# Moving the operands of the large products to start at 128 modulo 256 bytes, in a mixer and feed-forward kernel

## The chip, the cores and the metric

One core of one Trainium2 chip runs the kernel. The metric is the device time of one execution in microseconds (us); lower is better.

## What is computed

The reference is two blocks in a row on 512 tokens of width 1024, in float32. The first block normalises x (with 16 meta tokens in front), projects it, mixes it by a pooling mixer and by gated linear attention, and adds a mixture of 16 experts. The second block has two layers, each a gated feed-forward product, a hybrid attention mixer and a second feed-forward product:

```python
def swiglu(x, w_gate, w_up, w_down):
    return (jax.nn.silu(x @ w_gate) * (x @ w_up)) @ w_down
for l in range(DEPTH_2):
    x = x + 0.5 * swiglu(rms_norm(x, norm_ffn1[l]), ffn1_w_gate[l], ffn1_w_up[l], ffn1_w_down[l])
    x = x + hybrid_mixer(rms_norm(x, norm_mix[l]), w_in[l], w_proj_dil[l], w_proj_sb[l],
                         w_out[l], cos, sin)
    x = x + 0.5 * swiglu(rms_norm(x, norm_ffn2[l]), ffn2_w_gate[l], ffn2_w_up[l], ffn2_w_down[l])
return rms_norm(x, norm_final)
```

The feed-forward width is 2816, the input projection of each mixer is 1024 x 5120.

## The kernel before

The activations lie feature-major: a tile has 128 features on the partitions, 8 chunks c of them, and 512 tokens along the free dimension. Every large product is made from split operands: a float32 value is stored as a rounded part (`_hi`) and the rest (`_lo`), and the product is three matmuls, hi by hi, lo by hi and hi by lo, added in one PSUM bank. ScalarE makes the rounded part, VectorE the rest, for weights (`w_hi`, `w_lo`, a ring of three panels; lines 509 and 514) and for activations alike.

`product` (lines 547 to 560) is a panel of 128 output features: for each of 8 chunks c three matmuls, with a 128x128 piece of the weights stationary and a row of 512 tokens moving, 24 matmuls in all, called **wide** here. Its moving operands are `xg_hi`/`xg_lo` (the scaled x), `hid_hi_ff`/`hid_lo_ff` (the hidden layer), `y_hi`/`y_lo` (the gated sum in the second mixer), `heads_hi`/`heads_lo` (its attention outputs), and in the first mixer `y1_hi`/`y1_lo`, which the profile prints as `y_hi` and `y_lo` too. TensorE runs the panels in the fixed order of `weight_order`; each waits on a semaphore for its `w_lo`.

In the feed-forward stages 71 pairs of gate and up panels are made with seven half-size products instead of eight (`seven_pe` and `piece`, line 1866). Each of the seven is 4 chunks by three matmuls, with 256 tokens moving, called **narrow** here: 84 narrow matmuls per pair. Four of the seven take sums of quarters of x (`xs_hi`, `xs_lo`) as moving operand, three take quarters of `xg_hi`, `xg_lo` (`x_quarter`); three of the four and one of the three have sums of weights (`ws_hi`, `ws_lo`) stationary, the rest plain weights from the ring.

In the first block, the mixture of experts (`panel_products`, matmul at line 1347) has the roles swapped: weights from `w_hi`, `w_lo` move, 512 wide, and token tiles are stationary.

`sb(...)` allocates SBUF in the order in which the buffers are written down, each right behind the last, rounded up to 32 bytes; a buffer in an `ExitStack` that has been closed gives its place to what follows. So the start of each operand in a partition's memory is fixed by the sizes of all that stands before it. `xg_hi` and `xg_lo` have rows of L = 528 numbers (16 meta tokens and 512 tokens, 2112 bytes), of which all stages behind the first mixer read from column META = 16 on.

Start of the operands, in bytes modulo 256, worked out from the allocation:

| operand | before | after the change |
|---|---|---|
| `w_hi`, `w_lo`, stationary (pieces 512 bytes apart) | 128 | 128 |
| `xg_hi`, `xg_lo` from the token columns, chunk c (rows of 2112 bytes) | 192, 0, 64, 128, and again | 128 for every c (rows of 2048) |
| `hid_*_ff`, `xs_*`, `ws_*`, second mixer's `y_*` and `heads_*` | 224 | 128 |
| first mixer's `y1_*`; token tiles of the experts | 128 | 128 |

Of the kernel before, what the change touches and what calls it, by code (L numbers as in the profile page):

```python
# [159 lines left out]
def build(nc, dram, out, counts, final):  # L160
# [4 lines left out]
    with stack:  # L165
# [28 lines left out]
        x = sb(stack, "x", [P, DC, T])  # L194
        xg_hi = sb(stack, "xg_hi", [P, DC, L], F32R)
        xg_lo = sb(stack, "xg_lo", [P, DC, L], F32R)
        rstd = sb(stack, "rstd", [P, T])
# [58 lines left out]


        with ExitStack() as phase:

            weight_diag = sb(phase, "weight_diag", [P, TB, TOP_K, P])  # L260
# [3 lines left out]
        first_rstd = sb(stack, "first_rstd", [P, T])  # L264
        gain_pair = sb(stack, "gain_pair", [P, 2 * DC])


        with ExitStack() as phase:
            slot_of = sb(phase, "slot_of", [P, TB, TOP_K], U32)
            token_of = sb(phase, "token_of", [P, TILES], U32)  # L270
            weight = sb(phase, "weight", [P, TOP_K, TB, 1])
            with ExitStack() as ring:
                expert_raw = sb(ring, "expert_raw", [P, EXPERT_OWN, PANEL])
# [288 lines left out]
        def x_product(pe, key, emptied_by, emptied_key, ready=None, banks=l_banks):  # L562
            bank = claim(pe, banks, key, emptied_by, emptied_key)
            cols = panel_shape(panel_of[key])[1]
            product(pe, key, [bank[0:cols, :]], lambda c: [xg_hi[:, c, META:]], lambda c: [xg_lo[:, c, META:]], ready)

# [47 lines left out]
        def round_x(act, stage, c, factor):  # L614
            act.activation(xg_hi[:, c, META:], x[:, c, :], ACT.Copy, scale=factor).then_inc(*x_hi.done((stage, c)))

        def rest_of_x(dve, stage, c, factor):
            dve.wait_ge(*x_hi.upto((stage, c)))
            dve.scalar_tensor_tensor(xg_lo[:, c, META:], x[:, c, :], factor, xg_hi[:, c, META:].bitcast(F32),
                                     ALU.mult, ALU.subtract).then_inc(*x_lo.done((stage, c)))  # L620
# [25 lines left out]

        half = L // 2

        def mixer_1_pe(pe):
            def both(key, ready=None):  # L650

                l = claim(pe, l_banks, key, taken, (key, "l"))
                t = claim(pe, t_banks, key, taken, (key, "t"))
                product(pe, key, [l[:, 0:half], t[:, 0:half]],
                        lambda c: [xg_hi[:, c, 0:half], xg_hi[:, c, half:]],
                        lambda c: [xg_lo[:, c, 0:half], xg_lo[:, c, half:]], ready)

# [108 lines left out]
        def route_chunk(pe, c):  # L766

            w_high, w_low = split_memory(panel_of["route", 0])
            if c == 0:
                pe.wait_ge(*panel_lo.upto(panel_of["route", 0]))  # L770
                pe.wait_ge(*shaped.upto(("carry", N_CHUNK - 2, 1)))
            pe.wait_ge(*x_lo.upto(("m1", c)))
            for n, (w, part) in enumerate(((w_high, xg_hi), (w_high, xg_lo), (w_low, xg_hi))):
                m = pe.matmul(bank_s[:, 0, :], w[:, c * P:(c + 1) * P], part[:, c, META:],
                              start=c == 0 and n == 0, stop=c == DC - 1 and n == 2)
            if c == DC - 1:
                m.then_inc(*used.done(panel_of["route", 0]))

        def mixer_1_act(act):
            load_log_and_exp(act)  # L780
            act.wait_ge(*shaped.upto("meta_g"))
            round_value(act, "meta", xg_hi[:, :, 0:META], meta_g[:, :, :])
            act.wait_ge(loaded["gains"], 16)
# [103 lines left out]
        def mixer_1_dve(dve):  # L887
# [5 lines left out]
                "p (c o) -> p c o", o=1).to_broadcast([P, DC, META]), ALU.mult).then_inc(*shaped.done("meta_g"))  # L893
            rest_of_value(dve, "meta", xg_lo[:, :, 0:META], xg_hi[:, :, 0:META], meta_g[:, :, :])
            for c in range(DC):
# [10 lines left out]
            def take_both(key, dst, n=P):  # L906
                dve.wait_ge(*used.upto(panel_of[key]))
                dve.tensor_tensor(dst[0:n, 0:half], l_banks.of(key)[0:n, 0:half], all_rstd[0:n, 0:half],
                                  ALU.mult).then_inc(*taken.done((key, "l")))
                dve.tensor_tensor(dst[0:n, half:], t_banks.of(key)[0:n, 0:half], all_rstd[0:n, half:],  # L910
                                  ALU.mult).then_inc(*taken.done((key, "t")))
# [806 lines left out]
        def normalise_between_act(act):  # L1718
            load_log_and_exp(act)
            act.wait_ge(*shaped.upto("gain_pair"))  # L1720
            for half in range(2):
                ts = half_columns(half)
                for c in range(DC):
                    if c % 4 == 0:
                        act.wait_ge(*x_new.upto(("moe", 2 * half + 1, c // 4)))
                    act.activation(xg_hi[:, c, META:][:, ts], x[:, c, ts], ACT.Copy,
                                   scale=gain_pair[:, DC + c:DC + c + 1]).then_inc(
                        *x_hi.done(("n", c) if half else ("n_first_half", c)))
# [28 lines left out]
        def normalise_half_dve(dve, half, chunks):  # L1757
            ts = half_columns(half)
            for c in chunks:
                key = ("n", c) if half else ("n_first_half", c)  # L1760
                dve.wait_ge(*x_hi.upto(key))
                dve.scalar_tensor_tensor(xg_lo[:, c, META:][:, ts], x[:, c, ts], gain_pair[:, DC + c:DC + c + 1],
                                         xg_hi[:, c, META:][:, ts].bitcast(F32), ALU.mult, ALU.subtract).then_inc(
                    *x_lo.done(key))
# [74 lines left out]
        def x_quarter(part, k, t):  # L1839
            return part[:, 4 * k:4 * k + 4, META + half_t * t:META + half_t * t + half_t]  # L1840

# [1213 lines left out]
```

## Time and profile before

| | |
|---|---|
| median of three timed runs | 2575.88 us (2571.2 to 2576.82) |
| profiled execution: span from first to last instruction | 2569.2 us |
| profiled execution's own time | not recorded apart from the span; the median stands 6.7 us above the span |
| TensorE busy | 2477.2 us (96%) |
| VectorE, ScalarE, GpSimd busy | 1706.7, 1129.6, 422.1 us |
| mean granted TensorE clock | 0.989 of 2.4 GHz |

Matmuls are pipelined, so the mean duration of one is longer than the time from its start to the next one's start; that distance, called the **step** here, is what a matmul costs in a row of matmuls. It is read from start times. A busy TensorE is not a TensorE at its peak.

### The profile page before, as it was taken

Reading aid. Unit: us, or ns where it says so; the run is one execution under the profiler, and the core shown is the slowest. Engines: PE = TensorE matmul, PEld = TensorE weight load, DVE = VectorE, ACT = ScalarE, POOL = GpSimd, SP = SyncE. Lnnn points to the kernel's source line nnn. Section 1 sums busy time; section 2 is a strip of 40 time slices with the busy share of each in tenths; the row PEclk is TensorE's granted clock in tenths of the full one; section 3 lists DMA queues with packets and bytes.
Section 4 is the critical chain, followed back from the end, with each engine's and each line's share of the span. In section 5 each row is a group of like instructions: output and inputs, shape, how many; then the busy total and the mean of one; then the engine's idle time right before and its main releaser. Section 6 shows DMA issues by size and latency. Waiting matters only on the chain. (4 is left out here: it accounts for less than half of the span.)

```text
span 2569.2 us, 38480 instructions
## 1 busy us (share of the span) xinstructions
PE 2477.2 (96%) x15217; PEld 2130.2 (83%) x15217; DVE 1706.7 (66%) x2316; ACT 1129.6 (44%) x1586; POOL 422.1 (16%) x450
## 2 busy tenths in 40 slices
PE   7997996999999999999999999999999999999998
PEld 6876775889897878778898989999887777899996
DVE  5455996658686434467696878777743436687776
ACT  4344884335343233545353454444412255544443
POOL 0002111702012400012020102111050001111110
PEclk9998998999999999999999999999999999999999
DMA  4215995246454321125564546555332212465652
GB/s 144 66 58 198 385 413 203 83 143 162 139 127 133 98 80 55 64 91 156 144 172 129 124 134 166 145 158 140 119 110 84 67 42 90 131 157 150 159 142 72
DMA packets 120713, 348.69 MB, mean 136 GB/s; under 512 B 16066, under 2 KB 21074, under 8 KB 120274
## 3 DMA queue, kind: packets, MB, share of 16 engines
q1 hardware_dynamic: 81634, 245.48, 28.5%
q0 software_dynamic: 38032, 98.06, 16.4%
q8 instruction: 125, 2.05, 0.3%
q10 hardware_dynamic: 864, 2.62, 0.3%
q14 instruction: 58, 0.48, 0.1%
HBM read 331.95 MB, written 12.58 MB: 134 GB/s over the span
## 5 line engine op out<-in xcount | busy, mean ns | idle before, releaser
L514 DVE TENSOR_TENSOR w_lo<-w_raw,w_hi 128x1024 fp32r<-128x1024 f32 (+2 forms) x353 | 422.7, 1198 | 141.2 <-ACT w_hi L509 139.5
L509 ACT ACTIVATE w_hi<-w_raw 128x1024 fp32r<-128x1024 f32 (+2 forms) x353 | 352.4, 1003 | 364.4 <-PE bank_l L558 342.4
L558 PE MATMUL bank_l<-xg_hi,w_hi 128*128 128x512 f32 (+1 forms) x1008 | 395.8, 393 | 17.5 <-DVE w_lo L514 15.5
L558 PE MATMUL bank_l<-xg_lo,w_hi 128*128 128x512 f32 (+1 forms) x1008 | 389.8, 387 | 0.0
L558 PE MATMUL bank_l<-xg_hi,w_lo 128*128 128x512 f32 (+1 forms) x1008 | 387.5, 384 | 0.0
L558 PE MATMUL bank_l<-hid_hi_ff,w_hi 128*128 128x512 f32 x704 | 279.8, 397 | 4.2 <-DVE hid_lo_ff L644 4.2
L558 PE MATMUL bank_l<-hid_hi_ff,w_lo 128*128 128x512 f32 x704 | 278.7, 396 | 0.0
L558 PE MATMUL bank_l<-hid_lo_ff,w_hi 128*128 128x512 f32 x704 | 276.6, 393 | 0.0
L2009 ACT ACTIVATE ws_hi<-ws_raw 128x1024 fp32r<-128x1024 f32 x142 | 150.6, 1061 | 276.2 <-DVE ws_raw L2131 148.7
L558 PEld LDWEIGHTS bank_l<-xg_hi,w_hi 128*128 128x128 f32 x1008 | 190.0, 189 | 64.8 <-DVE w_lo L514 15.5
L1869 PE MATMUL bank_s<-xs_hi,ws_hi 128*128 128x256 f32 x852 | 241.4, 283 | 1.0 <-DVE ws_lo L2098 1.0
L1869 PE MATMUL bank_s<-xs_lo,ws_hi 128*128 128x256 f32 x852 | 240.7, 283 | 0.0
L1869 PE MATMUL bank_s<-xs_hi,ws_lo 128*128 128x256 f32 x852 | 240.3, 282 | 0.0
L558 PEld LDWEIGHTS bank_l<-xg_lo,w_hi 128*128 128x128 f32 x1008 | 190.0, 188 | 40.4 <-issue 2.2
L558 PEld LDWEIGHTS bank_l<-xg_hi,w_lo 128*128 128x128 f32 x1008 | 190.4, 189 | 39.3
L2098 DVE TENSOR_TENSOR ws_lo<-ws_raw,ws_hi 128x1024 fp32r<-128x1024 f32 x142 | 173.9, 1225 | 46.1 <-ACT ws_hi L2009 39.1
L2258 DVE TENSOR_TENSOR val_ff<-bank_l,rstd 128x512 f32<-128x512 f32 x96 | 66.3, 691 | 152.1 <-PE bank_l L558 127.3
L1869 PEld LDWEIGHTS bank_s<-xs_hi,ws_hi 128*128 128x128 f32 x852 | 162.3, 191 | 2.2 <-DVE ws_lo L2098 1.6
L1869 PEld LDWEIGHTS bank_s<-xs_hi,ws_lo 128*128 128x128 f32 x852 | 162.8, 191 | 0.0
L1869 PEld LDWEIGHTS bank_s<-xs_lo,ws_hi 128*128 128x128 f32 x852 | 162.6, 191 | 0.0
L558 PEld LDWEIGHTS bank_l<-hid_hi_ff,w_hi 128*128 128x128 f32 x704 | 132.2, 188 | 36.2 <-DVE hid_lo_ff L644 6.3
L558 PEld LDWEIGHTS bank_l<-hid_hi_ff,w_lo 128*128 128x128 f32 x704 | 132.2, 188 | 33.1
(440 smaller groups left out, 5467.4 us busy)
## 6 DMA issues: line engine op xcount, KB each, us to landing
ws_raw<-in_ff_up POOLq DMA_DIRECT2D x213, 256.0 KB, 4.1
w_raw<-in_ff_gate SPq DMA_DIRECT2D x88, 512.0 KB
expert_raw<-in_experts SPq DMA_DIRECT2D x81, 512.0 KB, 18.7
w_raw<-in_in SPq DMA_DIRECT2D x80, 512.0 KB
w_raw<-in_ff_down SPq DMA_DIRECT2D x64, 512.0 KB
ws_raw<-in_ff_gate POOLq DMA_DIRECT2D x71, 256.0 KB, 5.5
up_raw<-in_ff_up SPq DMA_DIRECT2D x71, 256.0 KB, 2.9
w_raw<-in_out SPq DMA_DIRECT2D x24, 512.0 KB
```

What stands on the lines that cost most here:

```text
L509: act.activation(split_memory(i)[0], split_part(i), ACT.Copy).then_inc(*panel_hi.done(i))
L514: dve.tensor_tensor(lo, split_part(i), hi.bitcast(F32), ALU.subtract).then_inc(*panel_lo.done(i))
L558: done = pe.matmul(dst, w[:, c * cols:(c + 1) * cols], moving, start=c == 0 and n == 0, stop=c == kc - 1 and n == 2)
L1869: done = pe.matmul(product_at[name], w[:, c * P:(c + 1) * P], m[:, c, :], start=c == 0 and n == 0, stop=c == DC // 2 - 1 and n == 2)
L2009: act.activation(ws_hi[:, 2 * pair:2 * pair + 2, :], raw_of_two(stage, j, pair), ACT.Copy).then_inc(*ws_high.done((stage, j, pair)))
L2098: dve.tensor_tensor(ws_lo[:, both, :], raw_of_two(stage, j, pair), ws_hi[:, both, :].bitcast(F32), ALU.subtract).then_inc(*ws_low.done((st ...
L2258: dve.tensor_tensor(val[:, :], l_banks.of(key)[:, :], rstd[:, :], ALU.mult).then_inc(*shaped.done((stage, g, m)))
```

## The change

No instruction is added, removed or moved on any engine, and no wait or semaphore differs. The two products that the first mixer makes of 528 tokens are cut as 256 and 272 columns instead of 264 and 264. All else is where operands lie. The scaled x of the first mixer gets its own names `in_hi` and `in_lo` with the old rows of 2112 bytes, in a scope that is closed at once; `xg_hi` and `xg_lo` take the same place with rows of 2048 bytes, and an unused buffer `behind_xg` fills what that frees, so that what follows keeps its place. Further unused buffers (`before_spent` of 160 bytes, `behind_weight` of 96 bytes) and `gain_pair`, now ahead, push the buffers of the later stages to the offsets of the table above.

```diff
         x = sb(stack, "x", [P, DC, T])
-        xg_hi = sb(stack, "xg_hi", [P, DC, L], F32R)
-        xg_lo = sb(stack, "xg_lo", [P, DC, L], F32R)
+        with ExitStack() as opening:
+            in_hi = sb(opening, "in_hi", [P, DC, L], F32R)
+            in_lo = sb(opening, "in_lo", [P, DC, L], F32R)
+        xg_hi = sb(stack, "xg_hi", [P, DC, T], F32R)
+        xg_lo = sb(stack, "xg_lo", [P, DC, T], F32R)
+        sb(stack, "behind_xg", [P, 2 * DC * META])
...
+        gain_pair = sb(stack, "gain_pair", [P, 2 * DC])
+        sb(stack, "before_spent", [P, 40])
         with ExitStack() as phase:
...
         first_rstd = sb(stack, "first_rstd", [P, T])
-        gain_pair = sb(stack, "gain_pair", [P, 2 * DC])
...
             weight = sb(phase, "weight", [P, TOP_K, TB, 1])
+            sb(phase, "behind_weight", [P, 24])
...
         def x_product(pe, key, emptied_by, emptied_key, ready=None, banks=l_banks):
             bank = claim(pe, banks, key, emptied_by, emptied_key)
+            of_hi, of_lo = (in_hi, in_lo) if key[0] in ("q", "r") else (xg_hi, xg_lo)
             cols = panel_shape(panel_of[key])[1]
-            product(pe, key, [bank[0:cols, :]], lambda c: [xg_hi[:, c, META:]], lambda c: [xg_lo[:, c, META:]], ready)
+            product(pe, key, [bank[0:cols, :]], lambda c: [of_hi[:, c, -T:]], lambda c: [of_lo[:, c, -T:]], ready)
...
-        half = L // 2
+        half = T // 2
...
-                product(pe, key, [l[:, 0:half], t[:, 0:half]],
-                        lambda c: [xg_hi[:, c, 0:half], xg_hi[:, c, half:]],
-                        lambda c: [xg_lo[:, c, 0:half], xg_lo[:, c, half:]], ready)
+                product(pe, key, [l[:, 0:half], t[:, 0:L - half]],
+                        lambda c: [in_hi[:, c, 0:half], in_hi[:, c, half:]],
+                        lambda c: [in_lo[:, c, 0:half], in_lo[:, c, half:]], ready)
...
         def x_quarter(part, k, t):
-            return part[:, 4 * k:4 * k + 4, META + half_t * t:META + half_t * t + half_t]
+            return part[:, 4 * k:4 * k + 4, half_t * t:half_t * t + half_t]
```

The other edits put `in_hi`/`in_lo` or `xg_hi`/`xg_lo` without META where the old names with META stood.

## Rows read from the trace of the kernel before

**Rows 1.** The page: busy time and share of the engines, and the granted clock in 40 slices.
```profile
PE 2477.2 (96%) x15217; PEld 2130.2 (83%) x15217; DVE 1706.7 (66%) x2316; ACT 1129.6 (44%) x1586; POOL 422.1 (16%) x450
...
PEclk9998998999999999999999999999999999999999
```
**Rows 2.** Busy time by engine in three stretches of the second block (start:end, length, busy).
```profile
439.00:800.00 361.00, 357.88 (x2119) 314.99 (x2118) 269.59 (x337) 150.94 (x207) 93.85 (x87) 1.00 0.45 125
800.00:1150.00 350.00, 345.20 (x2089) 273.37 (x2088) 167.89 (x243) 131.70 (x196) 54.19 (x33) 1.00 0.27 85
1150.00:1510.00 360.00, 357.91 (x2314) 323.78 (x2313) 277.18 (x363) 165.47 (x229) 56.32 (x78) 1.00 0.53 140
```
**Rows 3.** TensorE's groups by line and form: busy us, mean ns, idle before.
```profile
L558 PE MATMUL bank_l<-xg_hi,w_hi 128*128 128x512 f32 x920 | 368.8, 401 | 2.0 <-DVE xg_lo L619 2.0
...
L558 PE MATMUL bank_l<-hid_hi_ff,w_hi 128*128 128x512 f32 x704 | 279.8, 397 | 4.2 <-DVE hid_lo_ff L644 4.2
...
L1869 PE MATMUL bank_s<-xs_hi,ws_hi 128*128 128x256 f32 x852 | 241.4, 283 | 1.0 <-DVE ws_lo L2098 1.0
...
L1869 PE MATMUL bank_s<-xs_hi,w_hi 128*128 128x256 f32 x284 | 80.2, 282 | 0.0
...
L558 PE MATMUL bank_l<-y_hi,w_hi 128*128 128x512 f32 x192 | 77.7, 405 | 0.4 <-DVE y_lo L644 0.4
...
L558 PE MATMUL bank_l<-heads_hi,xg_hi 128*128 128x512 f32 x32 | 13.5, 422 | 3.5 <-DVE gates L2760 2.3 <-DVE part L2796 1.1
...
L558 PE MATMUL bank_s<-xg_hi,w_hi 128*128 128x512 f32 x24 | 9.5, 396 | 2.1 <-DVE xg_lo L1762 2.1
...
L558 PE MATMUL bank_t<-xg_hi,w_hi 128*128 128x512 f32 x16 | 6.3, 392 | 0.0
```
**Rows 4.** TensorE's timeline (start us, duration us): panels of `xg`, then of `hid`.
```profile
467.08 0.40 PE L558 MATMUL bank_l<-xg_lo,w_hi 128*128 128x512 f32 x1
...
533.36 0.39 PE L558 MATMUL bank_l<-xg_hi,w_lo 128*128 128x512 f32 x1
533.59 0.40 PE L558 MATMUL bank_l<-hid_hi_ff,w_hi 128*128 128x512 f32 x1
...
578.16 0.40 PE L558 MATMUL bank_l<-hid_hi_ff,w_lo 128*128 128x512 f32 x1
```
**Rows 5.** TensorE's timeline: three output panels of the first mixer (operands `y1_*`), and what follows each.
```profile
175.11 0.40 PE L558 MATMUL bank_l<-y_hi,w_hi 128*128 128x512 f32 x1
...
180.60 0.40 PE L774 MATMUL bank_s<-xg_hi,route_parts 128*128 128x512 f32 x1
...
193.60 0.39 PE L558 MATMUL bank_l<-y_hi,w_hi 128*128 128x512 f32 x1
...
199.04 0.40 PE L774 MATMUL bank_s<-xg_hi,route_parts 128*128 128x512 f32 x1
...
205.93 0.39 PE L558 MATMUL bank_l<-y_hi,w_hi 128*128 128x512 f32 x1
...
211.39 0.39 PE L774 MATMUL bank_s<-xg_hi,route_parts 128*128 128x512 f32 x1
```
**Rows 6.** Two of these stretches: length, TensorE busy, clock, DMA share, GB/s.
```profile
175.00:181.00 6.00, 6.00 (x28) 1.00 0.38 130
...
205.00:211.00 6.00, 6.00 (x28) 1.00 0.00 0
```
**Rows 7.** TensorE's timeline: expert down products, both operands at 128.
```profile
311.35 0.39 PE L1347 MATMUL bank_s<-w_lo,ht_hi_tile 128*128 128x512 f32 x1
...
313.65 0.39 PE L1347 MATMUL bank_s<-w_hi,ht_lo_tile 128*128 128x512 f32 x1
```
**Rows 8.** TensorE's timeline: one round of 84 narrow matmuls, 48 from `xs`, then 36 from `xg`.
```profile
1685.00 0.28 PE L1869 MATMUL bank_s<-xs_hi,ws_hi 128*128 128x256 f32 x1
...
1690.73 0.28 PE L1869 MATMUL bank_t<-xg_hi,ws_hi 128*128 128x256 f32 x1
...
1694.96 0.28 PE L1869 MATMUL bank_s<-xs_hi,ws_hi 128*128 128x256 f32 x1
```

More of the change, by code:

```diff
@@ L614, in round_x @@
         def round_x(act, stage, c, factor):
-            act.activation(xg_hi[:, c, META:], x[:, c, :], ACT.Copy, scale=factor).then_inc(*x_hi.done((stage, c)))
+            act.activation((in_hi if stage == "in" else xg_hi)[:, c, -T:], x[:, c, :], ACT.Copy, scale=factor).then_inc(*x_hi.done((stage, c)))
         def rest_of_x(dve, stage, c, factor):
             dve.wait_ge(*x_hi.upto((stage, c)))
-            dve.scalar_tensor_tensor(xg_lo[:, c, META:], x[:, c, :], factor, xg_hi[:, c, META:].bitcast(F32),
+            hi, lo = (in_hi, in_lo) if stage == "in" else (xg_hi, xg_lo)
+            dve.scalar_tensor_tensor(lo[:, c, -T:], x[:, c, :], factor, hi[:, c, -T:].bitcast(F32),
                                      ALU.mult, ALU.subtract).then_inc(*x_lo.done((stage, c)))
@@ L773, in route_chunk @@
             for n, (w, part) in enumerate(((w_high, xg_hi), (w_high, xg_lo), (w_low, xg_hi))):
-                m = pe.matmul(bank_s[:, 0, :], w[:, c * P:(c + 1) * P], part[:, c, META:],
+                m = pe.matmul(bank_s[:, 0, :], w[:, c * P:(c + 1) * P], part[:, c, :],
                               start=c == 0 and n == 0, stop=c == DC - 1 and n == 2)
@@ L781, in mixer_1_act @@
             act.wait_ge(*shaped.upto("meta_g"))
-            round_value(act, "meta", xg_hi[:, :, 0:META], meta_g[:, :, :])
+            round_value(act, "meta", in_hi[:, :, 0:META], meta_g[:, :, :])
             act.wait_ge(loaded["gains"], 16)
@@ L893, in mixer_1_dve @@
                 "p (c o) -> p c o", o=1).to_broadcast([P, DC, META]), ALU.mult).then_inc(*shaped.done("meta_g"))
-            rest_of_value(dve, "meta", xg_lo[:, :, 0:META], xg_hi[:, :, 0:META], meta_g[:, :, :])
+            rest_of_value(dve, "meta", in_lo[:, :, 0:META], in_hi[:, :, 0:META], meta_g[:, :, :])
             for c in range(DC):
@@ L909, in take_both @@
                                   ALU.mult).then_inc(*taken.done((key, "l")))
-                dve.tensor_tensor(dst[0:n, half:], t_banks.of(key)[0:n, 0:half], all_rstd[0:n, half:],
+                dve.tensor_tensor(dst[0:n, half:], t_banks.of(key)[0:n, 0:L - half], all_rstd[0:n, half:],
                                   ALU.mult).then_inc(*taken.done((key, "t")))
@@ L1725, in normalise_between_act @@
                         act.wait_ge(*x_new.upto(("moe", 2 * half + 1, c // 4)))
-                    act.activation(xg_hi[:, c, META:][:, ts], x[:, c, ts], ACT.Copy,
+                    act.activation(xg_hi[:, c, ts], x[:, c, ts], ACT.Copy,
                                    scale=gain_pair[:, DC + c:DC + c + 1]).then_inc(
@@ L1761, in normalise_half_dve @@
                 dve.wait_ge(*x_hi.upto(key))
-                dve.scalar_tensor_tensor(xg_lo[:, c, META:][:, ts], x[:, c, ts], gain_pair[:, DC + c:DC + c + 1],
-                                         xg_hi[:, c, META:][:, ts].bitcast(F32), ALU.mult, ALU.subtract).then_inc(
+                dve.scalar_tensor_tensor(xg_lo[:, c, ts], x[:, c, ts], gain_pair[:, DC + c:DC + c + 1],
+                                         xg_hi[:, c, ts].bitcast(F32), ALU.mult, ALU.subtract).then_inc(
                     *x_lo.done(key))
```

## The prediction

> **What bounds the kernel now.** I read the page first, then busy time by stretches, then start times. TensorE is busy 2477.2 of 2569.2 us, and the granted clock is at its upper level, 2.4 GHz, in nearly every slice [rows 1]. In the second block, from 439 us to the end, the reader is to see how little room there is beside it: 357.88 busy of 361.00 us, 345.20 of 350.00 and 357.91 of 360.00, at a clock of 1.00, while VectorE, the next engine, has 277.18 of 360.00 us (77%) in the densest of the three [rows 2]. So the second block is as long as its matmuls, and a nanosecond off each is a nanosecond off the time. What one costs is not its printed duration (about 400 ns for a wide one [rows 3]) but the step from start to start.
>
> **What the steps show.** The stream of 512 columns at 2.4 GHz lasts 213.3 ns, of 256 columns 106.7 ns. The rest of a step is excess, and the rows show that it differs between operands of one shape:
> - `hid`, at residue 224: 533.59 to 578.16 are 191 steps of 44.57 us, 233.4 ns each [rows 4], excess 20.1.
> - `xg`, with rows of 2112 bytes that walk through the residues 192, 0, 64, 128: 467.08 to 533.36 are 286 steps, 231.8 ns [rows 4], excess 18.5.
> - `y1`, at 128 with rows of 2048 bytes and the same weight ring: 24 steps of 5.49, 5.44 and 5.46 us, that is 228.8, 226.7 and 227.5 ns [rows 5], mean 227.7, excess 14.4. This is the layout that the change gives to all the others.
> - the experts' products, both operands at 128 but with the roles swapped: 311.35 to 313.65 are 10 steps, 230.0 ns [rows 7].
>
> `y1` is the nearest row, with its loop, shapes and ring. The obvious objection is that its stage is quieter. In its first panel the DMA engines were busy for 0.38 of the time and in its last for 0.00 [rows 6], and the steps are 228.8 and 227.5: DMA explains 1.3 ns of 5.7 at most. The middle panel has its 226.7 throughout, the two others begin slower, after the three router matmuls that stand between the panels. The changed stages have no such matmuls between most panels, so I take 227.2, between the mean and the settled value.
>
> **The change, part by part.** *Wide products.* Counts are three matmuls per row: `xg` 920 + 24 + 16, less 48 of the first mixer's q and r, which keep the old rows, is 912, times three 2736; `hid` 704 x 3 = 2112; `y` 192 less 64 of `y1`, times three, 384; `heads` 32 x 3, and as many with plain ring weights, 192 [rows 3]. `xg` gains 4.6 ns x 2736 = 12.6 us; `hid` 6.2 x 2112 = 13.1; `y` and `heads`, at 224 like `hid` and costed like it, 6.2 x 576 = 3.6. Together 29.3 us. The bounds: 226.7 for all would give 32.0 (5.1 x 2736 = 14.0 and 6.7 x 2688 = 18.0); 230.0, the swapped case, 14.1 (1.8 x 2736 = 4.9 and 3.4 x 2688 = 9.1).
>
> *Narrow products.* There are 71 x 84 = 5964: 852 x 3 + 284 x 3 = 3408 from `xs` [rows 3], the other 2556 from `xg`. In one round the 48 from `xs` take 5.73 us, 119.4 ns a step, and the 36 from `xg` 4.23 us, 117.5 ns [rows 8]. No row has a narrow product with both operands at 128 throughout, so it is bounded. If each loses as many ns as a wide one, 6.2, `xs` goes to 113.2, and `xg`, taken to the same level, loses 4.3: 21.1 + 11.0 = 32.1 us. If the excess cannot go below the 13.3 that a settled wide one keeps (226.7 less 213.3), a narrow one takes 120.0, and the edit costs 0.6 x 3408 + 2.5 x 2556 = 8.4 us. I take the middle, 116.5, since the rows show the excess growing with the width (12.7 narrow, 20.1 wide, both at 224) and so only part of the loss should carry over: 2.9 x 3408 + 1.0 x 2556 = 9.9 + 2.6 = 12.5 us.
>
> *The rest.* The cut into 256 and 272 columns streams the same 528; nothing. VectorE, ScalarE and GpSimd read and write the moved buffers too; they are covered by TensorE with 23% to spare [rows 2], and if TensorE gets 2% faster they remain covered. DMAs keep their number and size. The experts' products already lay at 128. Nothing is added to any queue.
>
> The sum is 29.3 + 12.5 = 41.8 us. The profiled execution has a span of 2569.2 us, and would have 2527.4; the median of the runs is 6.7 us above that span, which I carry over: 2575.9 - 41.8 = 2534.
>
> **The rivals.**
> - *Narrow products settle at 120.* For it: 120.0 is the wide excess unchanged, and `xs` is at 119.4 already. Against it: `xg` steps of 117.5 show that less is possible. 29.3 - 8.4 = 20.9 us gained: 2555. The Trainium skill, TensorE: Matmul & The Clock Gate, section LDWEIGHTS, puts loading 128 weight columns at 128/1.2, 107 ns, which no operand's place alters; by it the narrow ones are bound by the weight load as much as by the stream. No row here shows the load alone.
> - *Narrow products lose as much as wide ones.* 29.3 + 32.1 = 61.4 us gained: 2514. For it: a conflict between two reads would be paid per instruction.
> - *No effect.* The step does not depend on the place, and `y1` is fast for something else in its stage. Then 2576. Against it: `xg` and `hid` differ by 1.6 ns in panels that follow each other, with equal shapes and equal load. The Trainium skill, same page, section Back-to-back issue gap, gives an isolated gap of N/2.4 + 2.5 ns, 215.8 for 512 columns, with no term for where operands lie; by it the change is worth nothing. The trace disagrees twice: no wide step is that short, and steps of one width differ.
> - *Slower: walking rows were the good layout.* In the second block the walking `xg` is faster than the fixed `hid` (231.8 to 233.4) and faster narrow than `xs` (117.5 to 119.4). If what helps is that the residue changes from chunk to chunk, fixing it costs `xg` 1.6 x 2736 = 4.4 us and 1.9 x 2556 = 4.9 us, and the rest, fixed before and after, gains nothing: 9.3 us slower, 2585. Against it: `y1` is fixed and the fastest of all. It decides if the other operands gain less than those 9.3 us.
>
> **How the numbers follow.** The forecast has a chance of 0.52, the narrow ones at 120 have 0.20, the full loss 0.15, no effect 0.07, slower 0.06. The range reaches from a little under the full-loss case (2514) to past the case at 120 with a wide gain somewhat smaller than forecast (2555, and 7 us more): 2512 to 2562, which leaves out about 0.15. About 0.2%, 5 us, is what a measurement of this kernel can tell from no change. Faster by more than that are the first three, 0.87; no effect 0.07 with 0.01 for a wide step of 230 beside narrow ones at 120 (14.1 - 8.4, under 6 us) makes same 0.08; slower 0.05.
>
> **What would show it.** In the changed profile: steps of `hid` panels down from 233.4 to about 227, of `xg` panels from 231.8 to the same value, a narrow round of 84 down from 9.96 us to about 9.8, TensorE still busy over 98% of the second block, its matmul counts unchanged, the first 439 us unchanged within 1 us. Wrong would be: `hid` steps still at 233, narrow rounds longer than 9.96, or the steps shorter but idle time of TensorE in front of waits for `w_lo`, which would say that VectorE has become the bound.

## The result, and the profile after

The change makes the kernel 0.7% faster, less than half of the gain that was forecast. The time goes from 2575.6 to 2556.3 us, which lies inside the forecast's wide range all the same. Two of the kernels further down had one run each at a lower granted clock (0.86 and 0.81, 2696.8 and 2828.49 us); those two runs are left out of every time below.

| | before | after |
|---|---|---|
| median of four timed runs, us | 2575.59 (2571.2 to 2576.82) | 2556.3 (2554.39 to 2558.39) |
| ratio, with its 95% interval | | 0.993 (0.9916 to 0.9943) |
| span of the profiled execution, us | 2569.2 | 2552.5 |
| its own time, us | | 2554.39 |
| TensorE busy, us | 2477.2 | 2455.8 |
| forecast for the change, us | | 2534.0 (2512 to 2562) |

The profiled execution of the changed kernel took 1.9 us more than its span. The spans differ by 16.8 us before rounding, the medians by 19.3.

The page of the changed kernel, with the lines that answer to [rows 1] and [rows 3]:

```profile
span 2552.5 us, 38480 instructions
...
PE 2455.8 (96%) x15217; PEld 2137.9 (84%) x15217; DVE 1708.3 (67%) x2316; ACT 1130.2 (44%) x1586; POOL 423.2 (17%) x450
...
PEclk9998998999999999999999999999999999999999
...
L564 PE MATMUL bank_l<-xg_hi,w_hi 128*128 128x512 f32 x872 | 346.0, 397 | 5.0 <-DVE xg_lo L627 4.8
```

The instruction counts are the same, the clock is the same in every slice, and TensorE alone lost busy time. Of the 920 matmuls that stood in one group before, 872 read the new `xg_hi`; the 48 of the first mixer's q and r now read `in_hi` and form a group of their own. The three stretches of [rows 2]:

```profile
439.00:800.00 361.00, 356.45 (x2123) 317.62 (x2122) 271.78 (x340) 153.04 (x210) 95.33 (x87) 1.00 0.46 128
800.00:1150.00 350.00, 345.19 (x2113) 278.26 (x2114) 170.48 (x245) 134.99 (x201) 53.48 (x32) 1.00 0.27 83
1150.00:1510.00 360.00, 356.72 (x2317) 326.55 (x2316) 278.06 (x363) 169.48 (x233) 57.38 (x79) 1.00 0.54 144
```

TensorE is still busy for more than 98% of each, and more matmuls fit into the same length: 2123 + 2113 + 2317 = 6553, where it was 2119 + 2089 + 2314 = 6522. VectorE is busy for 77% of the densest stretch, as before. In one place it does hold TensorE up more than before: the wait for `xg_lo` in the L564 line above was 2.0 us in [rows 3] and is 4.8 now, over the same three matmuls. The steps are read from start times:

```profile
1156.36 0.39 PE L564 MATMUL bank_l<-xg_hi,w_hi 128*128 128x512 f32 x1
...
1161.80 0.39 PE L564 MATMUL bank_l<-xg_hi,w_hi 128*128 128x512 f32 x1
...
1584.30 0.39 PE L564 MATMUL bank_l<-hid_hi_ff,w_hi 128*128 128x512 f32 x1
...
1589.74 0.39 PE L564 MATMUL bank_l<-hid_hi_ff,w_hi 128*128 128x512 f32 x1
...
1675.65 0.28 PE L1877 MATMUL bank_s<-xs_hi,ws_hi 128*128 128x256 f32 x1
...
1681.41 0.28 PE L1877 MATMUL bank_t<-xg_hi,ws_hi 128*128 128x256 f32 x1
...
1685.73 0.28 PE L1877 MATMUL bank_s<-xs_hi,ws_hi 128*128 128x256 f32 x1
```

A panel of 24 wide matmuls takes 5.44 us, whichever operand moves, `xg` or `hid`: 226.7 ns a step, the settled step of `y1` in [rows 5] and 6.7 ns under the 233.4 of `hid` in [rows 4]. The narrow round went the other way. It takes 10.08 us, against 9.96 in [rows 8]: 5.76 us for the 48 of `xs` and 4.32 us for the 36 of `xg`, 120.0 ns a step in both.

Added up over the whole trace, from each TensorE matmul's start to the next one's start, waits included, the difference lies here (differences are taken before rounding):

| group | before, us | after, us | difference | the prediction |
|---|---|---|---|---|
| wide, `hid`, 2112 | 498.4 | 485.0 | -13.4 | -13.1 |
| wide, `xg`, with 144 of the first mixer's q and r, 2880 | 678.6 | 669.2 | -9.3 | -12.6 |
| wide, second mixer's `y`, 384 | 90.8 | 88.7 | -2.2 | -2.4 |
| wide, `heads`, 192 | 55.1 | 55.2 | 0.0 | -1.2 |
| narrow, all 5964 | 710.2 | 718.8 | +8.6 | -12.5 |
| everything else | | | -0.5 | 0 |
| span | 2569.2 | 2552.5 | -16.8 | -41.8 |

So the wide products gave most of what was forecast (24.9 of 29.3 us), and the narrow ones cost 8.6 us where a gain of 12.5 was forecast. That is the prediction's first rival: 8.4 us lost and 2555 us in all.

### The profile page after: what moved, and what is told of

Read it like the earlier page. It is cut to its first block and busy times, and to the rows that moved or that the text cites. A ratio compares the mean times of both kernels' runs of the same rounds, so it can differ in the third digit from the quotient of the medians.

```text
span 2552.5 us, 38480 instructions
## 1 busy us (share of the span) xinstructions
PE 2455.8 (96%) x15217; PEld 2137.9 (84%) x15217; DVE 1708.3 (67%) x2316; ACT 1130.2 (44%) x1586; POOL 423.2 (17%) x450
## 5 line engine op out<-in xcount | busy, mean ns | idle before, releaser
L564 PE MATMUL bank_l<-xg_hi,w_hi 128*128 128x512 f32 x872 | 346.0, 397 | 5.0 <-DVE xg_lo L627 4.8
L564 PE MATMUL bank_l<-xg_hi,w_lo 128*128 128x512 f32 x872 | 339.7, 390 | 0.0
L564 PE MATMUL bank_l<-xg_lo,w_hi 128*128 128x512 f32 x872 | 339.6, 389 | 0.0
L564 PE MATMUL bank_l<-hid_hi_ff,w_hi 128*128 128x512 f32 x704 | 274.6, 390 | 4.6 <-DVE hid_lo_ff L652 4.6
L564 PE MATMUL bank_l<-hid_lo_ff,w_hi 128*128 128x512 f32 x704 | 274.1, 389 | 0.0
L564 PE MATMUL bank_l<-hid_hi_ff,w_lo 128*128 128x512 f32 x704 | 273.9, 389 | 0.0
L564 PEld LDWEIGHTS bank_l<-xg_hi,w_hi 128*128 128x128 f32 x872 | 163.7, 188 | 44.2 <-DVE xg_lo L627 6.1
L564 PEld LDWEIGHTS bank_l<-xg_hi,w_lo 128*128 128x128 f32 x872 | 163.7, 188 | 34.4
L564 PEld LDWEIGHTS bank_l<-xg_lo,w_hi 128*128 128x128 f32 x872 | 163.8, 188 | 34.1 <-issue 1.4
L564 PEld LDWEIGHTS bank_l<-hid_hi_ff,w_hi 128*128 128x128 f32 x704 | 132.2, 188 | 33.7 <-DVE hid_lo_ff L652 6.7
L564 PEld LDWEIGHTS bank_l<-hid_hi_ff,w_lo 128*128 128x128 f32 x704 | 132.2, 188 | 27.6
```

The costliest lines, as they stand in the source:

```text
L564: done = pe.matmul(dst, w[:, c * cols:(c + 1) * cols], moving, start=c == 0 and n == 0, stop=c == kc - 1 and n == 2)
```

## The experiments

**The question.** In the layout before, the narrow products of `xs` with `ws` had both operands at 224. Each round has three of them in a row, and from the second on their step was 119.8 to 120.0 ns already. After the change both operands lie at 128, and the step is 120.0. That suggests a reading which the prediction did not have: what counts is not the place of an operand, but the **distance** d between the start of the stationary operand and that of the moving one, modulo 256 bytes (written from -96 to +128 here). `hid` before the change stood at d = 128 - 224 = -96; all that the change moved is at d = 0 after it. The rivals are that the place counts (128 good, 224 bad), that the rows of 2048 bytes count and not the start, or that something in the surroundings of a stage counts.

All kernels below differ from the changed kernel or the one before by where buffers lie, and by nothing else (one of them also lets two scratch buffers share memory). Mean steps are taken over the matmuls that follow each other with the same pair of operands, leaving out steps of 260 ns and more. Where a timeline is shown, the step is the time between the first and the last row shown, over the count of matmuls between them.

**One half alone: rows of 2048 bytes.** The changed kernel without the buffers that move the later stages, so that only `xg` lies anew and `hid`, `xs`, `ws`, `y`, `heads` stay at 224:

```diff
-        gain_pair = sb(stack, "gain_pair", [P, 2 * DC])
-        sb(stack, "before_spent", [P, 40])
         with ExitStack() as phase:
...
         first_rstd = sb(stack, "first_rstd", [P, T])
+        gain_pair = sb(stack, "gain_pair", [P, 2 * DC])
...
-            sb(phase, "behind_weight", [P, 24])
```

> Only xg_hi and xg_lo get rows of 2048 bytes at 128; every later buffer stays at 224. Theory A (each operand pair settles at a step of its own, given by where the two lie; at 128 and 128 it is the stream plus 13.3 ns, for a wide and a narrow matmul alike): wide xg steps 231.8 to 226.7 ns, narrow xg by ring weights 117.4 to 120.0, narrow xg by ws (still 224) stays below 120; hid stays at 233.4. Sum of start-to-start time: wide xg -9 us, narrow xg +5 us, so about 4 us faster than before, 2571. Rival B (the gain comes from all buffers agreeing with one another, not from each pair): nothing gained at all here.

Measured: 2567.17 us, ratio 0.9965 (0.9951 to 0.9979), 8.5 us less than before where about 4 were expected. From its timeline, an `xg` panel and a `hid` panel:

```profile
1162.79 0.39 PE L562 MATMUL bank_l<-xg_hi,w_hi 128*128 128x512 f32 x1
...
1168.23 0.39 PE L562 MATMUL bank_l<-xg_hi,w_hi 128*128 128x512 f32 x1
...
1592.24 0.40 PE L562 MATMUL bank_l<-hid_hi_ff,w_hi 128*128 128x512 f32 x1
...
1597.84 0.40 PE L562 MATMUL bank_l<-hid_hi_ff,w_hi 128*128 128x512 f32 x1
```

24 steps of `xg` in 5.44 us are 226.7 each, and 24 of `hid` in 5.60 us are 233.3. Both belong to one kernel, one shape and one weight ring, so nothing that the whole kernel has in common is the cause. By groups the wide `xg` gained 11.9 us here (9 were expected), and the narrow products of `xg` with plain ring weights lost 5.2 us, as they did in the whole change (5.5): the gain and this loss come from the same edit.

**The other half alone.** The kernel before with only the later buffers moved to 128; `xg` keeps its rows of 2112 bytes:

```diff
+        gain_pair = sb(stack, "gain_pair", [P, 2 * DC])
+        sb(stack, "before_spent", [P, 40])
         with ExitStack() as phase:
...
         first_rstd = sb(stack, "first_rstd", [P, T])
-        gain_pair = sb(stack, "gain_pair", [P, 2 * DC])
...
             weight = sb(phase, "weight", [P, TOP_K, TB, 1])
+            sb(phase, "behind_weight", [P, 24])
```

> xg keeps its rows of 2112 bytes; all later buffers go to 128. Theory A: hid steps 233.4 to 226.7 ns (-13.4 us), y -2.2 us, narrow xs to 120.0 (+1.5 us), xg unchanged in both widths, so 14 us faster than before, 2561. With the run above the two parts add up to the whole change (4 + 14 = 18 of 19). Rival B: the parts do not add up, this one gains less than 8 us.

Measured: 2564.95 us, ratio 0.9961 (0.9947 to 0.9975). An `xg` panel and a `hid` panel, each from its first start to its 24th:

```profile
1069.04 0.40 PE L560 MATMUL bank_l<-xg_hi,w_hi 128*128 128x512 f32 x1
...
1074.37 0.39 PE L560 MATMUL bank_l<-xg_hi,w_lo 128*128 128x512 f32 x1
...
1597.92 0.39 PE L560 MATMUL bank_l<-hid_hi_ff,w_hi 128*128 128x512 f32 x1
...
1603.13 0.39 PE L560 MATMUL bank_l<-hid_hi_ff,w_lo 128*128 128x512 f32 x1
```

5.33 us over 23 steps are 231.7, and 5.21 us are 226.5. Now it is `hid` that is fast. The halves are worth 3.5 and 3.9 thousandths, together 7.4, and the whole 7.0: within the intervals they add up. Two things were not as expected, and 10.7 us were gained in place of 14. Wide `xg`, whose step did not change, took 2.8 us more, 2.4 of them in the waits for `xg_lo` (2.0 us before, 4.4 here). And the narrow products of `xg` with ring weights rose from 117.4 to 118.2 ns although neither of their operands was moved, so a narrow step also depends a little on the products beside it.

**`xs` and `ws` back at 224, all else as changed.**

```diff
+            sb(phase, "before_xs", [P, 24])
             xs_hi = sb(phase, "xs_hi",
```

> The whole change, but xs and ws pushed back to 224 by 96 unused bytes before xs. Theory A: narrow xs by ws (both at 224) back to 119.4 ns and xs by ring weights to 119.2, -1.5 us or so against the changed kernel; xg by ws below 120 again, -1.5 us; hid and wide xg keep 226.7. In all 2 to 3 us faster than the changed kernel, 2553. Rival C (the narrow ones got slower because the wide neighbours changed, not by their own place): narrow steps stay at 120.0, time as the changed kernel.

Measured: 2555.88 us, ratio 0.9922 (0.9905 to 0.9938), not to be told from the change itself. `xs` with `ws`, both at 224, has a step of 119.9 from the second product of a round on, where 120.0 stands with both at 128; the mixed pairs have 119.3 (d = -96) and 117.7 (d = +96). For the narrow products the place 224 is no worse than 128. As a way to win back the 8.6 us this was a miss: its two better pairs are worth (120.0 - 119.3) x 852 + (120.0 - 117.7) x 852 = 2.6 us of matmul starts, and all narrow groups together took 3.7 us less, which the times do not show.

**The ring at 192, everything else at 128.** If 128 is a good place for a moving operand, `hid` stays fast here; if the distance decides, it falls back, and `y1` needs a look of its own, since the same buffer in front of the ring moves `y1` as well, to 192:

```diff
         w_raw = sb(stack, "w_raw", [P, RAW, PANEL])
+        sb(stack, "before_w", [P, 16])
         w_hi = sb(stack, "w_hi", [P, SPLIT, PANEL], F32R)
...
-        sb(stack, "before_spent", [P, 40])
+        sb(stack, "before_spent", [P, 24])
```

> The whole change, but the weight ring w_hi and w_lo lies at 192 modulo 256 and the moving operands stay at 128. Theory A in the form that the two residues must agree: wide steps leave 226.7 and go to 230 to 234, +15 to +35 us, and narrow ones by ring weights leave 120.0 downwards. Rival D (only the moving operand's own place counts): wide steps stay at 226.7, time as the changed kernel, 2556.

Measured: 2580.32 us, ratio 1.0018 (1.0008 to 1.0028), a little slower than the kernel before. A panel of `y1` (23 steps) and one of `hid` (24 steps):

```profile
190.75 0.39 PE L565 MATMUL bank_l<-y_hi,w_hi 128*128 128x512 f32 x1
...
195.99 0.39 PE L565 MATMUL bank_l<-y_hi,w_lo 128*128 128x512 f32 x1
...
1601.69 0.39 PE L565 MATMUL bank_l<-hid_hi_ff,w_hi 128*128 128x512 f32 x1
...
1607.29 0.39 PE L565 MATMUL bank_l<-hid_hi_ff,w_hi 128*128 128x512 f32 x1
```

`hid` at 128, the place that the change chose, is at 233.3 again, with the weights now 64 bytes further on; `xg`, at 128 with its rows of 2048 bytes, has 233.3 as well, so it is not the rows either. `y1` has left 128 together with its weights and is fast (5.24 us over 23 steps, 227.8). This run decides between place and distance for the wide products.

**Everything at 192.** The counter-check: the same distance of zero as in the change, at another place. (`stat` moves to where unused bytes were, to make room.)

```diff
         x = sb(stack, "x", [P, DC, T])
+        sb(stack, "before_x", [P, 16])
...
-        sb(stack, "before_spent", [P, 40])
+        stat = sb(stack, "stat", [P, 2, 8])
+        sb(stack, "before_spent", [P, 24])
...
-                stat = sb(dilated, "stat", [P, 2, 8])
```

> The changed kernel with everything from x on 64 bytes further: ring, xg, hid, xs, ws and y all at 192. Theory A (only the distance counts): wide 226.7, narrow 120.0, time as the changed kernel, 2556. Rival H (the place 128 modulo 256 itself counts): wide steps above 230, time near 2575.

Measured: 2560.65 us, ratio 0.9945 (0.9928 to 0.9961). A `hid` panel of 24, and the narrow round of 84:

```profile
1591.40 0.39 PE L565 MATMUL bank_l<-hid_hi_ff,w_hi 128*128 128x512 f32 x1
...
1596.84 0.39 PE L565 MATMUL bank_l<-hid_hi_ff,w_hi 128*128 128x512 f32 x1
...
1672.67 0.28 PE L1878 MATMUL bank_s<-xs_hi,ws_hi 128*128 128x256 f32 x1
...
1682.75 0.28 PE L1878 MATMUL bank_s<-xs_hi,ws_hi 128*128 128x256 f32 x1
```

5.44 and 10.08 us: 226.7 and 120.0, the steps of the change to the tenth. Added up, the `hid`, `y` and narrow groups have the sums of the changed kernel within 0.1 us. The profiled span is 7.3 us longer than that of the change all the same, and all of it lies in the first block: the 2079th matmul in order of start, near the end of that block, starts at 445.4 us where it was 438.5, and from there to the end the two take 2114.4 and 2114.0 us. Seven other kernels of this section whose first block lies exactly as in the change start that matmul at 438.3 to 444.4 us, with one profiled execution each, so most of the 7 us is no more than what the first block differs by from one execution to the next. A small part for the place 192 is not ruled out.

**Four distances for the narrow products.** Three unused buffers before `hid`, `xs` and `ws` put `ws` at a chosen distance from `xs` and `xg`, and `hid` at a chosen distance from the ring, while all else stays as changed. The edit for `ws` 64 bytes below (`ws` at 64, `hid` at 160):

```diff
+            sb(phase, "before_hid", [P, 8])
...
+            sb(phase, "before_xs", [P, 56])
...
+            sb(phase, "before_ws", [P, 48])
```

The others have 32, 32, 16 (`ws` at d = +64, `hid` at +128), 16, 48, 32 (+128 and -64) and 40, 24, 8 (+32 and +96).

> The changed kernel with ws_hi and ws_lo 64 bytes further, at 192, xs and xg staying at 128, so the stationary operand lies 64 above the moving one in 4 of the 7 narrow products; hid at 0, 128 below or above the ring. Theory A (the distance between the two operands sets the step, and for narrow ones a distance of 64 is better than none): narrow steps by ws fall from 120.0 to between 113.4 and 117.8, 7 to 22 us in all; hid steps rise from 226.7 to 231 or more, +9 us or more. Rival E (only the ring's buffers matter, ws at any place gives 120): narrow by ws stays at 120.0.

> As the run before, with ws at 0 (128 from the moving operand) and hid at 192 (64 above the ring). Theory A: narrow steps by ws somewhere in 113 to 120, hid about 233. Rival E: 120.0.

> ws at 64 (64 below the moving operand), hid at 160 (32 above the ring). Theory A: narrow steps by ws differ from those at plus 64, in 113 to 121; hid between 226.7 and 235. Rival F (the step depends on the distance without its sign): same narrow steps as at plus 64.

> ws at 160 (32 above the moving operand), hid at 32 (96 below the ring). Theory A: narrow steps by ws in 113 to 120, and if the distance acts in units of 64 bytes they stay at 120.0; hid about 233.

Measured, one run each and so without an interval, beside a run of the kernel before of 2579.05 us: 2561.17, 2564.68, 2546.9 and 2566.95 us. The third stands out, and its narrow round shows why:

```profile
1670.03 0.28 PE L1880 MATMUL bank_s<-xs_hi,ws_hi 128*128 128x256 f32 x1
...
1674.11 0.28 PE L1880 MATMUL bank_s<-xs_hi,w_hi 128*128 128x256 f32 x1
...
1675.55 0.28 PE L1880 MATMUL bank_t<-xg_hi,ws_hi 128*128 128x256 f32 x1
...
1676.91 0.28 PE L1880 MATMUL bank_t<-xg_hi,w_hi 128*128 128x256 f32 x1
...
1679.79 0.28 PE L1880 MATMUL bank_s<-xs_hi,ws_hi 128*128 128x256 f32 x1
```

The first 36, from `ws` at d = -64, take 4.08 us, 113.3 ns each. The 12 behind them, from the ring at d = 0, take 1.44 us, 120.0 each; then 12 in 1.36 us, 113.3, and 24 in 2.88 us, 120.0. The step changes from one product to the next, as the distance of its operands does.

Put together with the other kernels, the mean steps in ns are:

| d, bytes | wide (512) | narrow (256) | read in |
|---|---|---|---|
| 0 | 226.7 to 227.2 | 120.0; with 224 and 224, among products at other distances, 119.5 to 119.8 | the changed kernel; all at 192; the kernel before and `xs` at 224 |
| +32 | not tried | 118.4 to 118.6 | `ws` +32 |
| +64 | 233.3 | 117.8 to 118.0; some panels 113.4 | ring at 192; `ws` +64 |
| +96 | 234.3 | 117.7 | `hid` at 32; `xs` at 224 |
| +128 | 232.5 | 118.5 to 119.1 | `hid` at 0; `ws` +128 |
| -96 | 233.4 | 119.3 to 119.7 | the kernel before; `xg` alone changed; `xs` at 224 |
| -64 | 231.2 | 113.3, or 117.8 | `hid` at 192; `ws` -64 |
| -32 | 233.3 | not tried | `hid` at 160 |

The kernel before fits in. Its walking `xg` went through d = -64, +128, +64 and 0, for which the table gives (231.2 + 232.5 + 233.3 + 226.7) / 4 = 230.9 where 231.9 was measured. One chunk in four was at the good distance by accident. The 1.0 ns between the two is not explained; here the distance changes every three matmuls.

**A version from the table: `ws` alone at 64.** The wide products keep d = 0, and the 3408 narrow matmuls with `ws` go to d = -64:

```diff
+            sb(phase, "before_ws", [P, 48])
             ws_hi = sb(phase, "ws_hi",
```

> The changed kernel with one more unused buffer of 192 bytes, so that ws_hi and ws_lo lie at 64, 64 bytes below the moving xs and xg; nothing else moves. Theory A (the distance, stationary minus moving: 0 is best for wide, minus 64 for narrow): steps of xs by ws and xg by ws 120.0 to 113.3 ns, 3408 x 6.7 = 22.8 us less than the changed kernel, about 2534; xg and xs by ring weights stay at 120.0, wide at 226.7. Rival G (the gain of the run with ws at 64 came with hid's place there): narrow stays at 120.

Measured: 2543.57 us, ratio 0.9883 (0.9867 to 0.99), where about 2534 was expected. From its timeline:

```profile
1671.98 0.28 PE L1878 MATMUL bank_s<-xs_hi,ws_hi 128*128 128x256 f32 x1
...
1676.06 0.28 PE L1878 MATMUL bank_s<-xs_hi,w_hi 128*128 128x256 f32 x1
...
1681.74 0.28 PE L1878 MATMUL bank_s<-xs_hi,ws_hi 128*128 128x256 f32 x1
```

36 in 4.08 us again, and the round of 84 in 9.76. The narrow groups took 698.8 us, 20.0 less than in the changed kernel, and the profiled span fell by 11.4. The other 8.6 us have two places. In the first 585 us, before any narrow matmul runs, this execution lost 6.6 us to that of the change: the 2079th matmul starts 5.0 us later, and behind a step of 2.3 us that both traces have (from 444.8 us here, from 439.8 in the change) the granted clock fell to 0.55 and wide steps to 427 ns, the lower level of 1.2 GHz, where the change stayed at 1.00. The edit moves only `ws`, which is not used there by any matmul. From the first narrow matmul to the end the time fell by 18.0 us, from 1974.5 to 1956.5. The other 2 us are in wide `hid`, which took 2.3 us more at a settled step of 227.1: 22 of its steps are above 245 ns, where it was 10. One of the added ones, with what VectorE does beside it:

```profile
1580.65 0.69 DVE L653 TENSOR_TENSOR hid_lo_ff<-val_ff,hid_hi_ff 128x512 fp32r<-128x512 f32 x1 [0.70 <-ACT hid_hi_ff L649]
...
1580.96 0.39 PE L565 MATMUL bank_l<-hid_hi_ff,w_lo 128*128 128x512 f32 x1
...
1581.39 0.19 PEld L565 LDWEIGHTS bank_l<-hid_hi_ff,w_hi 128*128 128x128 f32 x1 [0.47 <-DVE hid_lo_ff L653]
1581.39 0.50 PE L565 MATMUL bank_l<-hid_hi_ff,w_hi 128*128 128x512 f32 x1
```

VectorE ends `hid_lo_ff` at 1581.34, and the matmul behind the long step starts 0.05 us later. Eleven long steps of `hid` end like this, where it was four, and 11 of `xs` behind a `ws_lo`, where it was six. So the faster narrow products begin to run into VectorE.

**All narrow matmuls at -64.** Slots of the ring get 256 bytes more, and the panels of the seven-product pairs start 64 bytes lower in them than the others, so that the plain weights have d = -64 in narrow products and 0 in wide ones. To make room, `turning` shares the memory of `gained_sum`.

```diff
-        w_hi = sb(stack, "w_hi", [P, SPLIT, PANEL], F32R)
-        w_lo = sb(stack, "w_lo", [P, SPLIT, PANEL], F32R)
+        w_hi = sb(stack, "w_hi", [P, SPLIT, PANEL + 64], F32R)
+        w_lo = sb(stack, "w_lo", [P, SPLIT, PANEL + 64], F32R)
...
+            sb(phase, "before_ws", [P, 48])
...
-                    turning = sb(rope, "turning", [P, T])
+                    turning = gained_sum
...
-                return w_hi[:, ring_of[i], PANEL // 2:], w_lo[:, ring_of[i], PANEL // 2:]
-            return w_hi[:, ring_of[i], 0:kc * cols], w_lo[:, ring_of[i], 0:kc * cols]
+                at, n = 64 + PANEL // 2 - 16, PANEL // 2
+            else:
+                at, n = 64 - 16 * bool(by_seven(i)), kc * cols
+            return w_hi[:, ring_of[i], at:at + n], w_lo[:, ring_of[i], at:at + n]
```

> As the run before, and the ring's slots get 256 bytes of room in front (the rotation's scratch buffer in the second mixer shares a dead buffer to make space), so that the gate and up panels of the seven-product pairs lie at 64 too, while all other panels stay at 128. Theory A: every narrow step 113.3, 5964 x 6.7 = 40 us less than the changed kernel, about 2516 to 2518; wide 226.7. If VectorE or a DMA becomes the bound, TensorE shows waits in front of the narrow products and less is gained.

Measured: 2547.23 us, ratio 0.9899 (0.9883 to 0.9916): no better than `ws` alone, though 5964 narrow matmuls are at -64 and not 3408.

```profile
1670.02 0.28 PE L1880 MATMUL bank_s<-xs_hi,ws_hi 128*128 128x256 f32 x1
...
1674.26 0.28 PE L1880 MATMUL bank_s<-xs_hi,w_hi 128*128 128x256 f32 x1
...
1679.91 0.28 PE L1880 MATMUL bank_s<-xs_hi,ws_hi 128*128 128x256 f32 x1
```

The same 36 matmuls at the same distance take 4.24 us here, 117.8 ns a step, and the whole round of 84 takes 9.89 us, 117.7 a step. So the distance of a matmul's own operands is not all: at -64 there are two settled steps, 113.3 and 117.8. VectorE as a new bound, which also could have eaten the gain, is not what happened: the steps within the products are longer, and narrow steps above 245 ns add up to 4.2 us, against 3.4 in the change.

**Three of four at -64.** In the two runs before, the 113.3 appeared where products at -64 followed products at 0, and 117.8 where all were at -64. This kernel leaves one of the four kinds at 0, `xg` with the plain weights of the gate panels, and lowers the up panels only, in the ring as it is:

```diff
+            sb(phase, "before_ws", [P, 48])
...
-                return w_hi[:, ring_of[i], PANEL // 2:], w_lo[:, ring_of[i], PANEL // 2:]
+                return w_hi[:, ring_of[i], PANEL // 2 - 16:PANEL - 16], w_lo[:, ring_of[i], PANEL // 2 - 16:PANEL - 16]
```

> The run with ws at 64, and the up panels of the seven-product pairs 64 bytes lower in their ring slots (at 64; those slots' first halves are unused), while the gate panels stay at 128. Theory J (at distance minus 64 a narrow stream has two settled steps, 113.3 and 117.8, and stays in the one it enters; entered from steps of 120.0 it takes 113.3): ws steps 113.3, xs by the up panel 113.3 as well, xg by the gate panel 120.0; 852 x 6.7 = 5.7 us less than with ws alone, about 2538. Rival K (the whole round falls to 117.8 once two buffers are moved): ws and up steps 117.8, near 2550.

Measured: 2540.34 us, ratio 0.9862 (0.9845 to 0.9879).

```profile
1670.93 0.28 PE L1878 MATMUL bank_s<-xs_hi,ws_hi 128*128 128x256 f32 x1
...
1675.01 0.28 PE L1878 MATMUL bank_s<-xs_hi,w_hi 128*128 128x256 f32 x1
...
1676.37 0.28 PE L1878 MATMUL bank_t<-xg_hi,ws_hi 128*128 128x256 f32 x1
...
1680.61 0.28 PE L1878 MATMUL bank_s<-xs_hi,ws_hi 128*128 128x256 f32 x1
```

36 in 4.08 us and 12 in 1.36 us are both 113.3, the 36 behind them take 4.24 us (12 at 113.3 and 24 at 120.0 would be 4.24), and the round of 84 takes 9.68. The products at -64 that follow one at 0 are at the short step again, and here stay there through a second product (`xs` with the ring: mean 114.0, in 60 of 71 rounds at 113 and in 11 at 118). It has the lowest time of all. Its interval lies wholly below those of the change (0.9916 to 0.9943) and of all narrow products at -64; against `ws` alone (0.9867 to 0.99) the intervals overlap. The narrow groups took 2.2 us less than with `ws` alone, and not the expected 5.7, since waits for `ws_lo` grew further (17 long steps of `xs`, 11 with `ws` alone) and some rounds ran at the longer step.

A product at 0 in front fits what most rounds of these kernels do, but it was not varied by itself, and the traces show that it is not all. In the kernel with `ws` alone at 64, in a round whose 36 matmuls have one distance and follow a product at 0:

```profile
1214.07 0.28 PE L1878 MATMUL bank_s<-xs_hi,ws_hi 128*128 128x256 f32 x1
...
1216.68 0.28 PE L1878 MATMUL bank_s<-xs_hi,ws_lo 128*128 128x256 f32 x1
1217.03 0.39 PE L1878 MATMUL bank_s<-xs_hi,ws_hi 128*128 128x256 f32 x1
...
1217.37 0.28 PE L1878 MATMUL bank_s<-xs_hi,ws_lo 128*128 128x256 f32 x1
...
1218.43 0.28 PE L1878 MATMUL bank_s<-xs_hi,ws_lo 128*128 128x256 f32 x1
```

The first 23 steps take 2.61 us, 113.5 ns each. Then comes one step of 0.35 us, and from 1217.37 on nine steps take 1.06 us, 117.8 each: the same operands, the same distance, and another step behind a short pause. The kernel with all narrow products at -64 has the reverse: behind a wait for `ws_lo`, 22 steps from 1180.12 to 1182.62 us have 113.6 ns, with no product at 0 in front. (This kernel also has wider ring slots than the other two; that was not varied by itself either.) So at -64 a pause can set either step, and which one it sets stays open.

## Why the prediction was wrong, point by point

- **TensorE's steps are the time: right, but for one wait.** TensorE stayed busy for over 98% of the three stretches, the counts did not change, and the five groups of the table add up to -16.3 us of the span's -16.8. The first 439 us stayed within 1 us, as forecast (the 2079th matmul starts at 439.1 us before and 438.5 after). What the prediction put at nothing is VectorE, "covered by TensorE with 23% to spare": that is an average, and at the start of three stages TensorE waited 4.8 us for `xg_lo` in place of 2.0.
- **The step depends on where the operands lie: right; on the residue as such: wrong.** The prediction took the residue of one operand as what matters (`y1`, at 128, as "the layout that the change gives to all the others"), and forecast by it. `y1` was fast at 128 because its weights lie at 128 too; with the ring at 192 it was fast at 192, and `hid` at 128 slow. For the wide products both readings forecast the same, so the term came out right for a reason that was only half understood.
- **Wide, `hid` 13.1 us: right** (13.4). The step fell from 233.4 to 227.0; 227.2 was taken.
- **Wide, `xg` 12.6 us: step right, sum too high** (9.3). 227.2 was taken and measured, from 231.9. The steps above 245 ns add up to 3.6 us more than before, which is what is missing, and 2.8 us of that are the wait for `xg_lo`. It goes with the speed of `hid`, whose products stand in front of those three stages: 4.4 to 4.8 us in the kernels with `hid` at 227 ns, 3.9 at 231.2, 2.6 at 232.5, and 2.0 to 2.3 in all those at 233.3 to 234.3. With only `xg` changed the wait was 2.3 us, and the group gained 11.9. So faster `hid` products give back 2.8 us in front of the next stage, since VectorE's chain there did not get shorter (its last four operations take 0.68 to 0.75 us each in both traces).
- **Wide, `y` and `heads` 3.6 us: 2.2.** `y` gave 2.2 of 2.4. The steps of `heads` fell from 233.2 to 229.9, but its 192 matmuls stand in short runs between which TensorE waits, and the gain was lost there: 55.1 us before and 55.2 after. They should not have been costed as if they stood in rows of matmuls.
- **Narrow, 12.5 us gained: the step that failed.** The prediction had the bracket of 113.2 to 120.0, and "I take the middle, 116.5, since the rows show the excess growing with the width and so only part of the loss should carry over". The step went to 120.0 in all four kinds, the upper end, and a round took 10.08 us, which the prediction had named as a sign of being wrong ("narrow rounds longer than 9.96"). That is 3.5 ns off for 5964 matmuls, 21 us of the 25 that are missing. The reason given for the middle was no measurement of what was asked, which is a narrow product at equal residues, and such rows were in the trace of before: 36 of each 48 matmuls of `xs` were `xs` with `ws`, both at 224. In the round of [rows 8] the first 12 of them have a step of 118.4 ns, the next 24 one of 119.9, and the 12 from the ring at 128 behind them 119.2; the 119.4 is the mean of all. Had the 48 been split product by product, and the pair been read as equal, the answer would have stood there.
- **The rivals.** "Narrow products settle at 120", with 0.20 and 2555 us, is what came. Its argument, that a narrow step cannot go below the excess of 13.3 that a wide one keeps, gave the right number here, and is false all the same: 113.3 is 6.6 ns above the 106.7 that the prediction gives for the stream. Its counter-argument, that the 117.5 of `xg` show that less is possible, was right. The "full loss" took 113.2 for the narrow step, which exists, but at another distance than the change gives.
- **The rule on weight loads** (the Trainium skill, TensorE: Matmul & The Clock Gate, section LDWEIGHTS: 107 ns for 128 weight columns). The page gives the time by the number of columns alone. By it the narrow products are bound by the load as much as by the stream, whatever the place. The runs have steps from 113.3 to 120.0 ns with the same load and the same stream, so the load may set a floor here, but it does not set the step. No run shows the load alone.
- **"Walking rows were the good layout", slower: half right.** The walk was the better layout for the narrow `xg`, whose 117.4 and 118.2 became 120.0, and 7.0 us were lost there (the rival said 4.9). For the wide ones it was the worse.
- **The carried-over 6.7 us** made no difference to the forecast gain. The spans differ by 16.8 us and the medians by 19.3; the 2.5 us between are within the spread of the runs.

## What to carry to other kernels

Where TensorE is the bound and matmuls stand in rows, compare the steps from start to start of products of equal shape, keyed by both operands, and put beside each the distance between the stationary and the moving operand's starts modulo 256 bytes: here equal residues were best for 512 columns and worst for 256, which wanted the stationary operand 64 bytes below. Steps of one pair also differ a little with the products beside it, so leave the first product of a row out when you read one. A layout that is good for one width can cost the other, so give each width its own buffers or its own place in a slot, and look for the pair in the trace that already has the new distance before you estimate between two bounds. And where TensorE gets faster in front of a stage that starts with another engine's result, count that wait anew: a share of busy time does not show it.

## What was not expected of the hardware

- A wide matmul at the upper clock has a step of 226.7 ns with both operands at the same residue modulo 256, and of 231.2 to 234.3 at the six other distances tried. The place itself changes nothing (226.7 at 128 and at 192).
- A narrow one has its longest step, 120.0 ns, where the wide one has its shortest. At all other distances tried it is shorter, down to 113.3 at -64.
- At one and the same distance there are two settled steps, 113.3 and 117.8 ns, which hold through whole products: at -64 between kernels (`ws` alone, and all narrow ones), and at +64 between panels of one kernel (the one with the ring at 192). One pause of 0.35 us inside a row of equal matmuls was enough to change from one to the other. What chooses between them is open.
- The first block, up to the 2079th matmul, took 438.3 to 444.4 us in eight profiled executions of kernels that are laid out alike there (granted clock from 165 to 439 us: 0.93 in the change, 0.91 with `ws` alone at 64). Two spans alone therefore misjudge an edit of the second block: for `ws` at 64 they give 11.4 us, and the stretch from the first narrow matmul on gives 18.0.
